# Padding every SBUF buffer of a two-layer encoder kernel to a multiple of 64 bytes per partition

## What is computed

```python
for layer in range(2):
    h = rms_norm(x, norm_mix[layer])
    if layer == 0:
        x = x + mixer_gla_sb(h, ...)   # gated linear attention (4 heads) | stick-breaking attention (8 heads)
    else:
        x = x + mixer_swa(h, ...)      # sliding-window attention, 16 query heads, 4 key heads, sinks, bias
    h = rms_norm(x, norm_ffn[layer])
    u = h @ w_up[layer]                # 1024 -> 5632
    c = conv_b + sum(pad(u)[:, i:i+T] * conv_w[i] for i in range(3))
    g, val = split(c, 2)
    x = x + (gelu(g) * val) @ w_down[layer]   # 2816 -> 1024
return rms_norm(x, norm_final)
```

## The kernel before

| buffer | bytes per partition | begins at | beyond a multiple of 128 by |
|---|---|---|---|
| `h_hi`, `h_lo` | 16,384 each | 32,896 and 49,280 | 0 |
| `w_hi` x2, `w_lo` x2 | 4,096 each | 82,048 to 94,336 | 0 |
| `par` | 1,616 | 98,432 | 0 |
| `rinv` | 2,048 | 100,064 | 96 |
| `rinv_col`, `var_col`, `mhalf`, `eps_col`, `gelu_warm` | 4 or 16 each | 102,112 to 102,240 | |
| `ssq`, `sq`, `ident`, `ones` | 2,048, 2,048, 512, 512 | 102,272 to 107,392 | 0 |
| `negtri`, `negones` (mixer 0) | 512 each | 107,904 and 108,416 | 0 |
| `ind16` | 8 | 109,952 | 0 |
| `qbT`, `kbT`, `vb`, `va`, `kg` to `sbE`, `sbS` | | 118,176 on | 32 |
| `sbH`, `sbL` | 5,120 each | 172,704 and 177,824 | 32 |
| `gE`, `gL` | 4,096 each | 182,944 and 187,040 | 32 |
| `oc_hi`, `oc_lo` | 16,384 each | 191,200 and 207,584 | 96 |
| `q1`, `k1`, ... (mixer 1) | | 107,392 on | 0 |
| `mx` to `negsink`: ten of 8 words or fewer | 32 each | 189,824 on | |
| `o1_hi`, `o1_lo` | 16,384 each | 190,144 and 206,528 | 64 |
| `y_hi`, `y_lo` (FFN) | 45,056 each | 107,392 and 152,448 | 0 |
| `us0`, `us1` | 2,056 each | 197,504 and 199,584 | |
| `cv0` to `cv3` | 2,048 each | 201,664 on | |

## Time and profile before

### The profile page before, as it was taken

The page is one execution under the profiler, slowest core; times in us unless marked ns, Lnnn a source line. Parts: engine busy times, 40 slices in busy tenths (PEclk is TensorE's granted clock), DMA queues, the critical chain, the costliest instruction groups (busy, mean ns, idle before and its releaser), DMA issues.

```text
span 1166.7 us, 15074 instructions
## 1 busy us (share of the span) xinstructions
PE 1139.4 (98%) x5402; PEld 925.3 (79%) x5402; DVE 654.0 (56%) x837; ACT 492.9 (42%) x714; POOL 8.6 (1%) x25
## 2 busy tenths in 40 slices
PE   8999999999999999999999999899999999999995
PEld 7776767778888888888888878688888888888884
DVE  5334433465677767774333465665777777763333
ACT  5457344653444344343233355544444444432220
POOL 1000000000000000000000000000000000000000
PEclk9999999999999999999999999999999999999997
DMA  5211111122232222323333312032322322223331
GB/s 224 72 55 55 58 51 54 37 91 94 91 104 90 100 98 90 105 65 95 93 97 122 108 60 93 29 107 90 103 95 90 108 90 92 90 78 96 99 85 72
DMA packets 31751, 102.92 MB, mean 88 GB/s; under 512 B 3537, under 2 KB 3682, under 8 KB 31714
## 3 DMA queue, kind: packets, MB, share of 16 engines
q1 hardware_dynamic: 30978, 100.17, 26.1%
q10 hardware_dynamic: 736, 2.24, 0.6%
HBM read 99.84 MB, written 2.10 MB: 87 GB/s over the span
## 4 chain that ended last, share of the span: by engine, by line
PE 60%; issue 31%; ACT 4%; DVE 3%; DMA 1%; POOLq 0%; POOL 0%; ACTq 0%; DVEq 0%; SPq 0%
PE ps L1157 18%; PE ps L1159 17%; PE ps L1158 17%; PE ps L1321 2%; PE ps L1308 2%; PE ps L1329 1%; ACT pr L814 1%; ACT w_hi L599 1%; PE ps L1380 1%; DVE w_lo L837 1%; DMA x<-xT 1%; PE ps L1452 1%; DVE sc L1108 1%; DVE mx L1118 0%; DVE x L1145 0%
## 5 line engine op out<-in xcount | busy, mean ns | idle before, releaser
L599 ACT ACTIVATE w_hi<-w_raw 128x1024 fp32r<-128x1024 f32 (+1 forms) x203 | 198.1, 976 | 518.6 <-PE ps L1159 518.6
L837 DVE TENSOR_TENSOR w_lo<-w_raw,w_hi 128x1024 fp32r<-128x1024 f32 (+1 forms) x205 | 229.8, 1121 | 247.1 <-ACT w_hi L599 241.0
L1157 PE MATMUL ps<-h_hi,w_hi 128*128 128x512 f32 x896 | 356.1, 397 | 6.7 <-DVE w_lo L837 2.1
L1159 PE MATMUL ps<-h_hi,w_lo 128*128 128x512 f32 x896 | 350.3, 391 | 0.0
L1158 PE MATMUL ps<-h_lo,w_hi 128*128 128x512 f32 x896 | 350.1, 391 | 0.0
L1157 PEld LDWEIGHTS ps<-h_hi,w_hi 128*128 128x128 f32 x896 | 168.9, 188 | 46.7 <-issue 10.9
L1159 PEld LDWEIGHTS ps<-h_hi,w_lo 128*128 128x128 f32 x896 | 169.0, 189 | 36.0
L1158 PEld LDWEIGHTS ps<-h_lo,w_hi 128*128 128x128 f32 x896 | 169.1, 189 | 34.8 <-issue 1.2
L1157 PE MATMUL ps<-y_hi,w_hi 128*128 128x512 f32 x352 | 136.9, 389 | 0.0
L1158 PE MATMUL ps<-y_lo,w_hi 128*128 128x512 f32 x352 | 136.9, 389 | 0.0
L1159 PE MATMUL ps<-y_hi,w_lo 128*128 128x512 f32 x352 | 136.9, 389 | 0.0
(11 more groups left out here) (178 smaller groups left out, 1054.1 us busy)
## 6 DMA issues: line engine op xcount, KB each, us to landing
w_raw<-w_up SPq DMA_DIRECT2D x88, 512.0 KB, 3.2
w_raw<-w_mix SPq DMA_DIRECT2D x53, 512.0 KB, 3.2
w_raw<-w_down SPq DMA_DIRECT2D x32, 384.0 KB, 3.1
w_raw<-w_down SPq DMA_DIRECT2D x32, 320.0 KB, 2.9
out<-x SPq DMA_DIRECT2D x8, 256.0 KB, 2.2
x<-xT SPq DMA_DIRECT2D x2, 512.0 KB, 8.0
x<-xT ACTq DMA_DIRECT2D x2, 512.0 KB, 8.1
bias_sb<-bias ACTq DMA_DIRECT2D x1, 512.0 KB, 4.2
```

The lines of the kernel that those rows point to most:

```text
L599: s.activation(w_hi[r % SPL][:, 0:cols], w_raw[r][:, 0:cols], ACT.Copy).then_inc(w_hi_ready, 1)
L837: v.tensor_tensor(w_lo[r % SPL][:, 0:cols], w_raw[r][:, 0:cols], w_hi[r % SPL][:, 0:cols].bitcast(F32), ALU.subtract).then_inc(w_lo_ready, 1)
L1157: mm(dst, w[0], m[0], start=first, stop=False, skip_group_check=shared)
L1159: return mm(dst, w[1], m[0], start=False, stop=last, skip_group_check=shared)
```

## The change

Only `sb` changes. Behind a buffer whose size is 1 to 8 words (of 4 bytes) above a multiple of 16 words it takes another one of 8 words, named `<name>_pad`, which no instruction touches. With places given out at multiples of 32 bytes this makes the next buffer begin at a multiple of 64. No instruction is added, removed or moved, and no order or wait is changed; addresses change.

```diff
+import math
@@
         def sb(name, shape, dt=F32, where=ctx):
-            return where.enter_context(nc.sbuf_tensor(name, shape, dt))
+
+            tile = where.enter_context(nc.sbuf_tensor(name, shape, dt))
+            words = math.prod(shape[1:]) * (2 if dt is BF16 else 4) // 4
+            if 0 < words % 16 <= 8:
+                where.enter_context(nc.sbuf_tensor(name + "_pad", [P, 8], F32))
+            return tile
```

## The result

The changed kernel takes **1175.02 us** (median of 5 runs, 1171.86 to 1176.29) against 1167.84: ratio 1.0061, 95% interval 1.0047 to 1.0074, so 0.6% slower. That is beyond the 0.3% that a measurement of this kernel can tell, and above the range of the prediction (1165.6 to 1172.0). Its profiled execution took 1176.29 us.

A forecast was written before the change was run, and what follows sets the result against it. PE was taken to bound the kernel, strictly in both FFNs. The terms 2.3 - 0.9 - 0.1 summed to +1.3 us, forecasting 1169.1 us against the median of 1167.84, with a range of 1165.6 to 1172.0.

The forecast's parts named there:

- What bounds the kernel: Both FFNs: PE busy for the whole of each stretch, so every nanosecond of their matmuls is one of kernel time.
- The term of `y`: Down stages: 1056 matmuls with `y` moving, 2.2 ns dearer each at `o1`'s rate, +2.3 us; bounds 0 and +7.1.
- the order of the rates is that of the remainders to 128: Float32r matmuls: rates of 226.7 to 233.4 ns rank by the moving operand's address modulo 128, not 64.
- The term of `oc`: 192 matmuls with `oc` moving, from 96 to 64 beyond a multiple of 128, -0.9 us; bounds 0 and -1.3.
- `sbH`, `sbL`: Buffers moved from 32 beyond to a multiple of 128: at most -0.14 us, counted as -0.1.
- Plain float32: Mixer 1 operands: products take 0.43 us each, twice the float32r time, whatever the place; 0.
- DVE and ACT: Operations cost the same at either place, 0; in the mixers 0.5 us either way allowed, from some 170 operations.
- Rival 3: `y`'s new place is bad because chunks longer than 128 bytes count: +6.1 us, 1173.9 us, chance 0.13.
- Rivals 1 and 2: First: a multiple of 64 is enough, 1166.4 us, chance 0.20. Second: places make no difference, 1167.8 us, chance 0.08.
- Rival 4: Late mixer 0: a dip of the granted clock added or removed, 1.8 us either way; with the rest, chance 0.07.
- The rule of 16-byte lines: SBUF has 16-byte lines; buffers begin at multiples of 32 before and after, so lines fill alike and nothing changes.
- The sign that I had named: If `o1` (same place modulo 512) or unmoved `h` changed its rate, the moving operand's place isn't the cause.

The follow-up runs named there:

- the sweep: 64 probes added behind the last matmul of the kernel before, moving and stationary operands each shifted 0 to 224 bytes in steps of 32; equal offsets gave 226.7 ns.

## Why the prediction was wrong

- **What bounds the kernel:** right. PE's nanoseconds in the down stages came out one for one, 3.5 us in each.
- **The term of `y`, +2.3 us: this is the step that failed.** "I take the row of `o1`, the same remainder to 128": the row had the right matmul, but the remainder to 128 wasn't what made its rate. Measured: 1056 x (233.3 - 226.7) = +7.0 us, where the upper bound of that step was 7.1. What made `o1`'s rate was its distance of 64 from the weights modulo 256; `y` went to a distance of 192.
- **Its ground, "the order of the rates is that of the remainders to 128":** four buffers, with the weights at one place in all of them. Such rows can't tell the place from the distance to the weights, and I didn't ask what the second operand's place was. With the distances it would have been seen that `y` goes to one (192) that no row of before had, and the bounds 0 and +7.1 would have stood with nothing in favour of 2.3.
- **The term of `oc`, -0.9:** 0.8, right by luck: the reason was wrong, and its new remainder happened to give it `o1`'s distance of 64 too. `o1` and `h` unchanged: as said.
- **`sbH`, `sbL`, -0.1:** the steps of `sfx` add up to 20.93 us where it was 20.97, so less than half of that.
- **Plain float32, 0:** mixer 1 takes 93.96 us where it took 93.90. But the row was misread. L1210 is one call of the kernel, and the trace has two records of 0.43 us for it; so one such product takes 0.86 us, nearly four float32r steps and not two.
- **DVE and ACT, 0, and 0.5 either way in the mixers:** they are busy for the same time within 0.4 us. The allowance counted some 170 operations, where the mixers have some 460 in the trace, which at 3 ns each would be 1.4 us; the forecast didn't hang on it. These terms weren't run alone.
- **Rival 3** came close to the time (1173.9 against 1175.02), and had the price (7.1) and the rate (over 230.9), at a chance of 0.13. That is luck too: its mechanism, longer chunks of the moving operand's own address, is refuted, for at a multiple of 512 `y` is as slow. Rivals 1 and 2 fall: `y` didn't keep its 226.7. Rival 4 took 1.7 us in the profiled execution, and is scatter.
- **The rule of 16-byte lines** (the Trainium skill, "Advanced Engine Details and Errata", section "Memory Cachelines"): by that rule, no change. The trace disagrees: `y` takes 233.3 ns against 226.7, and it begins at a multiple of 32 bytes in both kernels.
- **The sign that I had named,** that `h` unmoved must keep its rate, couldn't catch the error in this change, because the weights didn't move either. It took a run that moved them.

## What to carry to other kernels

For float32r matmuls with 128 weight and 512 moving columns, in threes with other weights each time as here, put the moving buffers at the same address modulo 256 bytes as the stationary ones, counted per partition, whatever that address is (it held with both at 128 and with both at 192 beyond a multiple of 256, and for all eight equal offsets of the sweep): here it was worth 6.6 of 233.3 ns, 3% of each such matmul. Other data types weren't tried, and at 256 columns distance 0 isn't the best, so measure there. A rule like "align to 64" can undo this by accident, since any small buffer ahead in the allocation shifts all that follow; look up the addresses of both operands, and compare the distance between starts in stages of the same pattern. And where a few rows of a trace rank by a property, ask which second property ranks them alike before taking a value from it.

## What was not expected of the hardware

- The distance effect itself: 226.7 ns at 0, 228.9 at 64, 232.8 to 234.6 at the other whole multiples of 32, up to 240.0 off them.
- Not one of the distances tried brings a float32r step of 512 columns below 226.7 ns, 13.4 above 512 columns at 2.4 GHz; at 256 columns one distance (192) gives 113.3 where distance 0 gives 119.6. Where these 13.4 ns come from is open, and they are in every one of the 4128 three-part matmuls of this kernel that have activations moving 512 wide.
- The same distance can be the best at one width and near the worst at another: 0 at 512 and at 256 columns.
- Fewer weight columns (64, 32) make the step at distance 0 longer, 230.0 and 231.7 ns, not shorter.
